# The opening of the first block as part of one fixed schedule, with the index products of a query tile in blocks of four pairs

## What is computed

```python
hn = rmsnorm(h, norm_mix_g[l])
proj = jnp.einsum('bsd,de->bse', hn, w_in[l])
(a_q, a_k, a_v, i_q, i_k, i_w, b_cq, b_ckv, b_kr, g_a, g_b) = jnp.split(proj, IN_OFFSETS, axis=-1)
i_q = apply_rope(i_q...) * (IDX_DIM ** -0.5)
i_k = apply_rope(rmsnorm(i_k, idx_k_norm_g[l])[:, :, None, :], ...)[:, :, 0, :]
c_q = rmsnorm(b_cq, q_a_norm_g[l])
c_kv = rmsnorm(b_ckv, kv_a_norm_g[l])
k_rope = apply_rope(b_kr[:, :, None, :], ...)[:, :, 0, :]
# of the index branch, per block of 128 queries:
dots = jnp.einsum('bqhd,bsd->bqhs', qib, ki)          # 8 heads of 64
iscore = jnp.einsum('bqh,bqhs->bqs', wib, jax.nn.relu(dots))
_, idx = lax.top_k(iscore, topk)                      # selects keys for branch A
```

## Time and profile before

| | us |
|---|---|
| three timed runs | 2382.78, 2398.24, 2399.77 (median 2398.24) |
| the profiled execution, its own time | 2388.91 |
| its span in the trace | 2387.1 |

### The profile page before, as it was taken

How to read it: one execution, slowest core, us unless ns; L and a number is a source line. 1 busy time by engine, 2 the same in 40 slices (tenths; PEclk the granted TensorE clock), 3 DMA queues, 4 the chain that set the end, 5 groups by cost and what they waited for, 6 DMA issues and landing times.

```text
span 2387.1 us, 36382 instructions
## 1 busy us (share of the span) xinstructions
PE 2259.3 (95%) x12401; PEld 1819.8 (76%) x12401; DVE 1266.4 (53%) x2684; ACT 910.5 (38%) x1812; POOL 224.5 (9%) x194
## 2 busy tenths in 40 slices
PE   5789999999999999999999799999999999999997
PEld 2445776677888888999999777777777677888885
DVE  4645887755773774543343455544445655443442
ACT  4324544444441444332232334444344443322332
POOL 0000003342000003000000000012100031000001
PEclk8878999999999999999999999999999999999998
DMA  2101121123453343234333232234423323332331
GB/s 77 43 12 44 37 64 41 54 81 101 145 153 102 97 121 107 87 92 126 88 88 104 66 89 79 75 89 107 98 82 99 86 84 97 89 111 83 94 101 59
DMA packets 400422, 205.88 MB, mean 86 GB/s; under 512 B 68988, under 2 KB 393960, under 8 KB 400316
## 3 DMA queue, kind: packets, MB, share of 16 engines
q1 hardware_dynamic: 400316, 204.52, 30.1%
HBM read 202.21 MB, written 14.80 MB: 91 GB/s over the span
## 4 chain that ended last, share of the span: by engine, by line
PE 64%; issue 17%; DVE 4%; ACT 2%; POOL 1%; DMA 0%; DVEq 0%; POOLq 0%; SPq 0%; ACTq 0%
PE acc L1085 35%; PE acc L1290 15%; PE acc L1139 5%; PE sco L1325 2%; PE acc L1389 2%; PE acc L1385 1%; DVE w_lo L2009 1%; PE sco L1178 1%; PE sco L1365 1%; PE acc L1222 1%; PE acc L1365 0%; PE sco L1345 0%; PE acc L1209 0%; PE sco L1199 0%; PE acc L1199 0%
## 5 line engine op out<-in xcount | busy, mean ns | idle before, releaser
L1547 ACT ACTIVATE w_hi<-raw 128x512 fp32r<-128x512 f32 (+4 forms) x660 | 374.6, 615 | 696.5 <-PE acc L1085 662.0
L2009 DVE TENSOR_TENSOR w_lo<-raw,w_hi 128x512 fp32r<-128x512 f32 (+4 forms) x660 | 423.8, 682 | 168.1 <-ACT w_hi L1547 165.3
L1085 PE MATMUL acc<-xn_hi,w_hi 128*128 128x512 f32 (+2 forms) x1480 | 452.7, 344 | 12.8 <-DVE xn_lo L2036 10.0
L1085 PE MATMUL acc<-xn_lo,w_hi 128*128 128x512 f32 (+2 forms) x1480 | 451.9, 344 | 0.0
L1085 PE MATMUL acc<-xn_hi,w_lo 128*128 128x512 f32 (+2 forms) x1480 | 450.5, 343 | 0.0
L1085 PEld LDWEIGHTS acc<-xn_hi,w_hi 128*128 128x128 f32 (+1 forms) x1480 | 256.1, 188 | 58.1 <-issue 14.3
L1085 PEld LDWEIGHTS acc<-xn_hi,w_lo 128*128 128x128 f32 (+1 forms) x1480 | 255.7, 189 | 34.3 <-issue 0.4
L1085 PEld LDWEIGHTS acc<-xn_lo,w_hi 128*128 128x128 f32 (+1 forms) x1480 | 255.2, 188 | 34.6 <-issue 1.0
L1085 PE MATMUL acc<-hid_hi,w_hi 128*128 128x512 f32 (+1 forms) x832 | 260.9, 348 | 6.3 <-DVE hid_lo L2431 6.3
L1085 PE MATMUL acc<-hid_lo,w_hi 128*128 128x512 f32 (+1 forms) x832 | 262.6, 350 | 0.0
L1085 PE MATMUL acc<-hid_hi,w_lo 128*128 128x512 f32 (+1 forms) x832 | 261.3, 348 | 0.0
(11 more groups left out here) (354 smaller groups left out, 2998.8 us busy)
## 6 DMA issues: line engine op xcount, KB each, us to landing
raw<-in_w_ffn_in SPq DMA_DIRECT2D x176, 256.0 KB, 3.0
raw<-in_w_in SPq DMA_DIRECT2D x118, 256.0 KB, 3.1
raw<-in_w_up SPq DMA_DIRECT2D x88, 256.0 KB, 3.0
raw<-in_w_ffn_out SPq DMA_DIRECT2D x32, 384.0 KB, 3.4
raw<-in_w_gate SPq DMA_DIRECT2D x48, 256.0 KB, 3.1
raw<-in_w_ffn_out SPq DMA_DIRECT2D x32, 320.0 KB, 3.8
raw<-in_w_out SPq DMA_DIRECT2D x32, 256.0 KB, 3.0
bias<-grids_dram SPq DMA_DIRECT2D x64, 128.0 KB, 2.9
```

Of the source, the lines that this page charges most:

```text
L1085: mm = pe.matmul(acc[0:m, 2 * slot + b, 0:size], w[slot][:, t, 0:m], x[:, place(t), c:c + size], start=(t == 0 and w is w_hi and x is xh), ...
L1547: act.activation(w_hi[slot][:, a:b, :], raw[slot][:, a:b, :], ACT.Copy).then_inc(S[f"hi_ready{slot}"], parts)
L2009: dve.tensor_tensor(w_lo[slot][:, a:b, :], raw[slot][:, a:b, :], w_hi[slot][:, a:b, :].bitcast(F32), ALU.subtract).then_inc(S[f"split{slot ...
```

## The change

All phases from the norm of x to `ready` are gone from `PHASES`. `setup` shrinks, and the rest becomes the beginning of `work_of_front`'s list:

- x is squared and rooted per token by ACT (four tiles of 128 x 1024), scaled per token by DVE before its transposition, and transposed once raw (for `h`) and once scaled. The scaled transposition of k tile k+2 stands behind the matmuls of k tile k of the first item; ACT takes the high part with the norm's gain, DVE the low part.
- The positions and the norm's gain are loaded from ACT's queue at its start, SP loads weights before the small vectors. DVE makes the angles of table a in `setup`, those of table b behind the first rotation's inputs. The tables' lines, the vectors, the small norms and the rotations stand between or within items.
- The nine items of the opening are items 0 to 8 of the schedule, so `kv0` is now item 9, and all later items change slots. `q1` stands ahead of `kv1`.
- The index products: for a query tile, the products of both heads of an item follow each other, into `sco[0:2]` and `acc[2:4]` in turn; four tiles in one block, a block behind `ckv`, `iq2`, `iq3` and the first gate `g0`. Three buffers hold ReLUs. The first product of a tile starts the scores (L2356 of the new file), so that they aren't set to zero.
- Rotations of the opening use POOL's cosine product and two DVE operations.

```diff
-PHASES = [("setup",), ("norm", "norm_mix_g", 1), ("prologue",), ("norm", "idx_k_norm_g", 1), ("norm", "q_a_norm_g", 1),
-          ("norm", "kv_a_norm_g", 1), ("rope",), ("index",), ("ready",),
+PHASES = [("setup",),
           ("front",), ("resplit", 1), ("proj_out", 1),
...
+    order.extend([("first", ik), ("xturn", 0), ("xturn", 1)])
+    for k in range(KT):
+        dense(ik, k, k + 1)
+        if k + 2 < KT:
+            order.append(("xturn", k + 2))
+        if k == 1:
+            order.append(("first", bkr))
+    order.extend([("now", ik), ("square", "ik"), ("xcopy", 0)])
+    whole(bkr, [("nsum", "ik"), ("vecs", 0), ("root", "ik")])
+    order.extend([("angles", 1), ("iw", 0)])
+    whole(cq0, [("sines", 0), ("lines", 0)])
+    whole(cq1, ("rope", ik))
+    order.append(("square", "cq"))
+    whole(iq0, [("nsum", "cq"), ("root", "cq"), ("rope", bkr)])
+    order.append(("hi", "cq"))
+    whole(iq1, [("rope", iq0), ("tables", 0)])
+    order.append(("causal", 0))
+    dots = [("dots", x) for x in range(16)]
+    whole(ckv)
+    order.extend([*dots[0:4], ("square", "ckv"), ("rope", iq1)])
+    whole(iq2, [("nsum", "ckv"), ("root", "ckv")])
+    order.extend([("hi", "ckv"), *dots[4:8], ("rope", iq2)])
+    whole(iq3)
+    order.extend(dots[8:12])
...
     dense(kv0)
+    order.extend([("now", kv0), ("rope", iq3)])
     dense(q0)
...
+    order.append(("now", q0))
+    whole(g0, [("rope", q0)])
+    order.extend(dots[12:16])
+    dense(q1)
+    order.extend([("now", q1), ("vturn", 0)])
     dense(kv1)
...
+    order.extend([("now", kv1), ("score", 0), ("lam", 0)])
...
+                def dots(x):
...
+                    if x >= 2:
+                        pe.wait_ge(S["relu_ready"], n.at("relu_ready", 2 * x - 2))
+                    for hh, bank in enumerate(dots_banks(x)):
+                        r = slice(64 * hh, 64 * hh + 64)
+                        mm = pe.matmul(bank, index_q[i % 2][r, P * j:P * j + P], index_keys[r, :], start=True, stop=True)
+                    mm.then_inc(S["dots_full"], 1)
```

More of the change, by code:

```diff
@@ L486, in events @@
         count, _, split = NORMS[phase[1]]
[L487 to L494, removed]
+        return 1, norm_events(count, split)
     if kind == "front":
@@ L834, in front_weights @@
                 slot, k = j % 2, k_of_item(j)
-                if kind == "bkv":
+                column = {"ik": "i_k", "bkr": "b_kr", "cq": "b_cq", "ckv": "b_ckv", "iq": "i_q"}.get(kind)
+                if column:
+                    first = IN1[column] + P * at - (64 if kind == "bkr" else 0)
+                    rows(slot, k, win1, first, tiles, {"ik": 72, "bkr": 96}.get(kind, P))
+                elif kind == "bkv":
                     load(slot, k, [(raw[slot][:, 0:1, 0:64], wuk[:, at:at + 1, :]),
@@ L920, in _ @@
[L920 to L939 removed]
+                    sp.dma_start(meta_tok, A["meta_tokens_2"]).then_inc(meta_in, 16)
@@ L1088, in item @@
                 mm.then_inc(S[f"item_done{slot}"], 1)
-            def squares(count, blk, rows=P):
-                for k in range(count):
-                    pe.wait_ge(S["sq_ready"], n.at("sq_ready", k + 1))
-                    for b, (c, size) in enumerate(segs(blk)):
-                        mm = pe.matmul(sco[:, 2 + b, 0:size], ones[0:rows, :], probs[0:rows, k % 2, c:c + size],
-                                       start=(k == 0), stop=(k == count - 1))
-                    mm.then_inc(S["sq_used"], 1)
             def sums(number):
@@ L1111, in sums @@
                         S["sq_used"], 1)
-            def partners(matrix, x, rows, bank):
-                pe.matmul(sco[0:rows, bank, 0:SEQ], matrix[0:rows, 0:rows], x[0:rows, META:T], start=True,
-                          stop=True).then_inc(S["turned"], 1)
             def front():
@@ new lines, in small_sum @@
+                def small_sum(name):
+                    first, count, rows, _ = SMALL[name]
+                    at = SMALL_ORDER.index(name)
+                    if at == 0:
+                        pe.wait_ge(x_copied, 6)
+                    else:
+                        pe.wait_ge(S["small_root"], n.at("small_root", at))
+                    for k in range(count):
+                        pe.wait_ge(S["small_sq"], n.at("small_sq", first + k + 1))
+                        mm = pe.matmul(sco[:, 3, :], ones[0:rows, :], small_square[k][0:rows, :], start=k == 0,
+                                       stop=k == count - 1)
+                    mm.then_inc(S["small_sum"], 1)
@@ new lines, in turn_index_weights, with make_lines @@
+                def turn_index_weights(j):
+                    taken(front_item("ik", 0))
+                    for t in range(4):
+                        mm = pe.transpose(sco[:, 1, 8 * t:8 * t + 8], key_raw[64:72, P * t:P * t + P], eye[64:72, 64:72])
+                    mm.then_inc(S["iw_full"], 1)
+                def make_lines():
+                    pe.wait_ge(load_in, 16 * TABLE_LOADS)
+                    pe.wait_ge(vec_copied, 1)
+                    for b in range(3):
+                        size = min(352, LINE - 352 * b)
+                        mm = pe.matmul(line_banks[b][:, 0:size], table, onehot[:, 352 * b:352 * b + size], start=True,
+                                       stop=True)
+                    mm.then_inc(lines_full, 1)
```

680 lines of the change are left out of this document (398 added, 282 removed).

## The result

| | before | changed |
|---|---|---|
| median of the timed runs, us | 2398.22 (2382.78 to 2399.77, 4 runs) | 2324.89 (2322.88 to 2330.18, 4 runs) |
| profiled execution, us (its span) | 2388.91 (2387.1) | 2325.94 (2323.8) |
| granted PE clock, mean of the span | 0.974 | 0.986 |
| first projection matmul / `score(0)`, us | 47.3 / 205.62 | 24.59 / 137.60 |
| from `score(0)` to the end, us | 2181.5 | 2186.2 |

The changed kernel is faster: ratio 0.9706, 95% interval 0.9666 to 0.9746. The two profiled executions lie 63.0 us apart, the medians 73.3: three of the four timed runs of the kernel before took some 2398 us, one 2382.78, and its profiled one 2388.91. What follows goes by the profiles. At `score(0)` the lead is 68.0 us, so nearly 5 us are given back behind it. Of the 68.0 us, 22.7 are there at the first projection matmul (47.3 against 24.59).

The account below looks back on a forecast made before the run. Opening bound by hand-overs between engines in successive phases. 22.6 + 14.1 + 84.4 + 12 + 3 = 136.1 us for `score(0)` against 205.6, so 2320; with a third of the median's offset 2323, range 2300 to 2350.

Parts of the forecast that it names:

- Step 1: Kernel start up to the first projection: DVE's angles wait for the positions, then x is scaled; 22.6 us.
- Step 2: First item (`ik`), transposes alternating with matmuls: two k tiles at low clock, six at full, a weight split between; 14.1 us.
- Steps 3 to 5: First item's end to `score(0)`: PE's work at full clock 84.4 us, new PE stalls 12, clock drop and queues 3.
- (a): Stall: the sum of squares of `ik` waits for DVE's copies of x tiles 2 and 3; 2.8 us.
- (b): Stall: `iq0` waits for its split, behind DVE's cosines and lines and the second angles; 1.5 us.
- (c): Stall: the rotation of `iq0` waits for the bank of `bkr`'s rotation, behind a reciprocal and two scalings; 1.2 us.
- (d): Stall: in each index block the third pair needs the first's ReLUs, late behind an ACT split; 3.6 us over four blocks.
- (e): Stall: `g0`'s weights wait behind the third index block's ReLUs and additions; 2.6 us.
- A: Rival: pairs of index products don't overlap in the opening; 10.6 us more, 2334 us; 7%.
- B: Rival: clock stays low for a third of the new opening; 2351 us, up to 2374 for more; 10%.
- C: Rival: clock low all the way to `score(0)`, which comes at 212 us; 2395 us, over 2422 if longer; 4%.
- D: Rival: fewer stalls than walked, positions early, no clock drop; 20 us better or more, 2300 or less; 9%.

Follow-up runs that it names:

- e4_angles_late: Changed kernel with DVE's position casts and first angles moved from before the scaling of x to behind the x copies; 2319.02 us.
- e3_singles_dealt: Changed kernel with its 32 index products dealt out singly, one ahead of each k tile, instead of pairs in blocks; timing only; 2340.06 us.
- e5_xcopy_early: Changed kernel with DVE's copies of the last two x tiles moved inside the first item, behind its fourth and sixth k tile; 2323.95 us.
- e6_slots_swapped: Changed kernel with the two weight slots of the first block exchanged, nothing added or moved; 2322.75 us.
- e2: Changed kernel with its 16 pairs of index products dealt out, one after every second k tile, instead of four blocks; timing only; 2325.35 us.
- the last three experiments: Changed kernel with angles later, x copies inside first item, slots exchanged, rounding later; then table-line work later, then later still: 2314.92, 2314.19, 2314.35 us.

## Why the prediction was right, point by point

The forecast was 2323 us, measured 2324.89; `score(0)` was put at 136.1, measured 137.6.

- **Step 1** (22.6 us, measured 24.59): order and releaser right, DVE behind angles behind positions. The term missed is the landing: 11.89 us, not 10. Casts and angles took 5.1 as taken; a reciprocal with its scale 0.86, not 1.03. e4_angles_late shows the mechanism: without the positions in the way the first projection comes at 16.79.
- **Step 2** (14.1, measured 12.9): two to three k tiles at the low clock, then full. What lowered it was the idle time of 8.79 us ahead: in e4_angles_late, with 0.92 us there, it didn't fall in this item. It rose again in the midst of transposes and projections. The Trainium skill ("TensorE: Matmul & The Clock Gate", Part 4: PE-mode transpose) says that transposes don't count as busy for the clock. The trace doesn't bear that out: in setup, where PE does hardly anything but transpose, eight fp32 transposes took 1.97 us at 5.28 and 1.06 us at 11.91. So the clock rose among transposes alone.
- **Steps 3 to 5** (84.4 + 12 + 3 = 99.4, measured 100.2 from 37.4 on). That it came within 1 us is three misses that offset each other: stalls of some 9.5 us instead of 12, 4.4 us for the clock instead of 3, and what is left, 86.3 us of PE's work, instead of 84.4. The blocks took 4.8, 7.9, 4.8 and 4.4 us (4.2 to 6 foreseen). Pairs: 16 x 1.06 was the row of before, and held at 0.96 to 1.06; e3_singles_dealt shows what it is worth. Stalls: (a) 2.75 against 2.8; (b) none against 1.5: the first half of the split was there at 65.4 us, PE came at 65.8; (c) 1.16 against 1.2; (d) 0.78, 2.37, 0.62 and 0.33 = 4.1 against 3.6, with the second block's cause not seen (I put it to ACT's split, it was the rounding of `ckv`); (e) 1.11 against 2.6. Clock: two drops, not one (0.54 from 43 to 50 us, 0.57 from 104 to 108), for 2.9 us by e5_xcopy_early and about 1.5 for the two pairs that took 1.86 and 1.71 us instead of some 1.0.
- **Behind `score(0)`** (up to 1 us, measured 4.7): the term that failed. I had written that the same items stand in the other slot, and given it no price. It has one at the end of the block, 325 us later, some 2.5 us by e6_slots_swapped. DVE's last split costs the 0.95 us foreseen: PE waits for it at 139.57 us. From `score(0)` to the last pair product it is 1.5 us in all (290.4 against 289.0), from there to the first residual 4.1, and behind that some 0.9 are won back, which is within what that part varies by.
- **Rivals.** A falls (pairs overlap: e2 against e3). B and C fall with a granted clock of 0.95 from 37.4 us to `score(0)`, the two drops included. D falls too: fewer stalls than walked, but the positions were late and the clock dropped twice.
- On the profiled execution's scale the forecast was 2320 and the measurement 2325.94: 1.5 us too little up to `score(0)`, some 4 behind it. That the median came within 2 us is luck in good part: 3 us were added for the offset of the old median, and the new one lies 1 us under its profiled execution.

## What to carry to other kernels

Pair 64-row products before thinking about where they stand: that is worth half of them, while blocks or dealing out differ by 2 us at most. After a schedule's rewrite, look at what a count has turned over, such as the buffer slot that the last item leaves to the next phase. And add up each engine's work in a stretch before adding up gains: three fixes worth 17 us at one point one by one gave 11 there together, while the second engine was over nine tenths busy on the way.

## What the hardware showed unasked

DVE and POOL hold each other up. The two halves of a weight split take 1.28 us alone and 2.36 with a POOL product of two SBUF operands beside them, which itself takes 1.68 instead of 1.27 (changed kernel, DVE, then POOL):

```profile
64.72 1.28 DVE L2166 TENSOR_TENSOR w_lo<-raw,w_hi 128x512 fp32r<-128x512 f32 x2
...
68.04 2.36 DVE L2166 TENSOR_TENSOR w_lo<-raw,w_hi 128x512 fp32r<-128x512 f32 x2
```

```profile
68.18 1.68 POOL L1087 TENSOR_TENSOR bias<-merged,aux 96x512 f32<-96x512 f32 x1 [5.46 <-DVE merged L2228]
...
115.16 1.27 POOL L1087 TENSOR_TENSOR bias<-merged,aux 128x512 f32<-128x512 f32 x1 [13.26 <-ACT merged L1670]
```

The Trainium skill ("SBUF — State Buffer", SBUF: two separate sides) has a pair of ports that DVE with two SBUF inputs and a POOL instruction that reads SBUF hold in turn, each for a whole instruction. The 1.08 us added here fit most of one POOL instruction of 1.27. The same pair of instructions takes 2.40 us at 77.96, again with a POOL product beside it. The one at 68.04 costs nothing in the changed kernel, since DVE then waits 0.80 us for ACT. In the last three experiments, where DVE is the fuller engine, it may count; that wasn't tried.
